# Two ways to lay out the output of a chunked linear recurrence: rows of tokens, or rows of value channels

## The chip, the cores and the metric

One core of one Trainium2 chip runs the whole program. The metric is the device time of one execution in microseconds (us), lower is better. TensorE (PE) multiplies, VectorE (DVE) and ScalarE (ACT) work on tiles in SBUF and in PSUM, GpSimd (POOL) does some small sums, and the queue of SyncE (SP) issues the weight loads. Each engine runs its own instruction list in order; semaphores tie the lists together.

## The reference, cut to what matters

The program is two transformer-like blocks in float32 on 256 tokens of 1024 channels, with some 215 MB of weights read once. The change touches one mixer of the second block, a two-directional gated linear recurrence ("HGRN2") with 4 heads of 128 value channels, in chunks of 32 tokens. It is summed over both directions, normed per token and head, scaled and gated:

```python
def step(state, inp):                     # per chunk of 32 tokens, per head
    qc, kc, vc, gc = inp
    bcum = jnp.cumsum(gc, axis=2)
    btot = bcum[:, :, -1:]
    qe = qc * jnp.exp(bcum)
    ke = kc * jnp.exp(-bcum)
    att = jnp.where(causal_in_chunk, jnp.einsum('bhtk,bhsk->bhts', qe, ke), 0.0)
    o = jnp.einsum('bhtk,bhkv->bhtv', qe, state) + jnp.einsum('bhts,bhsv->bhtv', att, vc)
    ...
def _hg_readout(o, g, norm_w):            # o is the sum of both directions
    o = o * lax.rsqrt(jnp.mean(o * o, axis=-1, keepdims=True) + EPS)
    o = o * norm_w ...
    return o * jax.nn.silu(g)
```

What follows the mixer is a product with an output matrix, and that wants its input with channels on the partitions.

## The kernel before, in words

**Staging.** All weight matrices stream through a ring of 4 raw tiles of 1 MB (`raw`). A list of "units" fixes their order. SP issues the load of a unit as soon as the unit four places ahead of it has been used. For most units ACT then makes a rounded high part (`whi`, line 1053), DVE the low part (`wlo`, line 1582), and PE takes three products per tile (lines 491 to 493). Units of kind "ada" are used raw: 16 small matmul records at line 592, after which ACT copies the bank out (line 1076). SP can load on only when PE has used them.

**The stretch with the recurrence.** After the gates are ready the program goes through eight slots n = 0 to 7, one per direction and head (`SLOT2`). In a slot PE does `within(n)` (line 837, attention inside a chunk), `adds(n)` (line 851, what each chunk adds to the state), `turn_kd` (line 825), and then one projection unit of 48 large matmuls. In the middle of that unit, and at its end in the last slots, it does `outputs(n-1)` (lines 862 and 867). DVE masks the attention (line 1987), runs the recurrence over the 8 chunk states (line 1995), splits weights (line 1582) and takes the output out of PSUM in `keep_o` (lines 1964 and 1966). `within(n)` waits for `keep_o(n-2)`, and `outputs(n)` for the states and for `keep_o(n-1)`.

`outputs` has, for one head and direction, two matmuls for the attention part (one per 128 tokens) and eight for the state part (one per chunk of 32 tokens). Before, the tokens are the rows of the result: the 32 queries of a chunk are the stationary operand and the 128x128 state streams past it. The four chunks of 128 tokens sit in four column groups of the array. A float32 matmul shows as two records in the trace, so these ten matmuls are 4 and 16 records.

**The stretch behind it.** Ten steps s = 0 to 9 of a windowed attention (the `na` steps) follow: scores (line 897), ACT's exponentials (1188), DVE's bias, maximum and scaling (2040 to 2051), PE's transposes (909) and the weighted sums (924). Each step carries up to two "ada" units, and from s = 5 on a projection by the output matrix (`evoB`), which reads the normed and gated recurrence output. The norm of that output runs in the first steps. Before: ACT squares and sums rows (line 1395) as heads become ready, and forms one factor per token and head; DVE applies it (line 2020, s = 0); PE waits for that in s = 1 and turns the result by eight transposes (line 938); DVE multiplies by the gate out of PSUM (line 2026, s = 1); ACT and DVE split it into high and low parts (lines 1458 and 2060, s = 2).

Of the kernel before, what the change touches and what calls it, by code (L numbers as in the profile page):

```python
# [22 lines left out]
P = 128  # L23
D = 1024
KT = D // P
S = 256
# [111 lines left out]
def build(nc, x, norm_gain, w_in, b_forget, lambda_q1, lambda_k1, lambda_q2, lambda_k2, subln_gain, sinks,  # L138
# [25 lines left out]
    with ExitStack() as ctx:  # L164
# [114 lines left out]
        ot = oT[:, :, :].rearrange("p h s -> p (h s)").rearrange("p (t j v) -> p t j v", t=NT, j=4)  # L279
# [206 lines left out]
        def _(pe):  # L486
# [368 lines left out]
            def outputs(n):  # L855
                d, j = 1 - n // 4, n % 4
                pe.wait_ge(att_set, min(n + 2, 8))
                pe.wait_ge(st_set, n + 1)
                if n:
                    pe.wait_ge(o_kept, n)  # L860
                for t in range(NT):
                    mm(psY[:, t * P:(t + 1) * P], ATTM[2 * (n // 4) + n % 2][:, t, :], hv[:, t, j * P:(j + 1) * P],
                       start=(t == 0), stop=False, skip_group_check=True)
                for t in range(NT):
                    for c in range(4):
                        cc = 4 * t + c
                        last = mm(psY[c * CH:(c + 1) * CH, t * P:(t + 1) * P], QE[d][:, j, cc * CH:(cc + 1) * CH],
                                  sq[:, n % 2, cc, :], start=False, stop=True, skip_group_check=True)
                last.then_inc(o_done, 1)
# [58 lines left out]
            for s in range(NA + 2):  # L928
                if s >= 2:
                    na_turn(s - 2, 0)  # L930
                if s < NA:
                    na_scores(s)
                if s == 1:
                    pe.wait_ge(hg_gated, 1)
                    for j in range(4):
                        for t in range(NT):
                            n = (j % 2) * NT + t
                            last = nc.tensor.transpose((psX, psY)[j // 2][:, n * P:(n + 1) * P], ot[:, t, j, :],
                                                       ident[:, :])
                    last.then_inc(sub_sum, 1)  # L940
                ada(f"na{s}a")
                if s >= 2:
                    na_turn(s - 2, 1)
                if s in EVO_AT:
                    if EVO_AT[s] == 0:
                        pe.wait_ge(hg_ready, 1)
                    project(SPAN["evoB"][EVO_AT[s]], Hhi, Hlo, base=4)
                ada(f"na{s}b")
                if s >= 2:
                    na_weigh(s - 2)  # L950
# [81 lines left out]
        def _(act):  # L1032
# [358 lines left out]
            def square_output(j):  # L1391

                act.wait_ge(o_kept, 5 + j)
                for t in range(NT):
                    ins = nc.scalar.activation(kk[:, j // 2, 2 * (j % 2) + t, 0:P], ot[:, t, j, :], ACT.Square,
                                               accum_out=lbc[:, 0, 4 * t + j:4 * t + j + 1])
                return ins

# [12 lines left out]
            for n, u in enumerate(SLOT2):  # L1411
# [18 lines left out]
                else:  # L1430
                    square_output(0)
                    square_output(1)
# [15 lines left out]
            for s in range(NA + 2):  # L1448
                if s >= 2:
                    keep_turned(s - 2, 0)  # L1450
                if s == 0:
                    square_output(2)
                    step(square_output(3))
                    step(nc.scalar.activation(lbc[:, 1, :], lbc[:, 0, :], ACT.Ln, bias=eps[:, 0:1], scale=1.0 / P))
                    nc.scalar.activation(lbc[:, 2, :], lbc[:, 1, :], ACT.Exp, scale=-0.5).then_inc(sub_inv, 1)
                elif s == 2:
                    act.wait_ge(hg_gated, 2)
                    nc.scalar.copy(Hhi[:, 4:8, :], oT[:, :, :]).then_inc(hg_high, 1)
# [3 lines left out]
                if s < NA:  # L1462
                    exps(NG + s, [(pn[:, s % 2, i, :], psS[:, 2 * (s % 2) + i, :]) for i in range(2)], False)
                keep_rows(f"na{s}b")
# [94 lines left out]
        def _(dve):  # L1559
# [398 lines left out]
            def keep_o(n):  # L1958
# [3 lines left out]
                o = psY[:, 0:S].rearrange("p (t v) -> p t v", t=NT)  # L1962
                if n < 4:
                    ins = V.tensor_copy(ot[:, :, j, :], o)
                else:
                    ins = V.tensor_tensor(ot[:, :, j, :], ot[:, :, j, :], o, ALU.add)
# [48 lines left out]
            def scale_output():  # L2015

                dve.wait_ge(sub_inv, 2)
                o = ot.rearrange("p t j v -> p (t j) v")
                r = lbc[:, 2, :].rearrange("p (a b) -> p a b", b=1).to_broadcast([P, 8, P])
                then(V.tensor_tensor(o, o, r, ALU.mult), hg_gated, 1)  # L2020

            def norm_output():

                dve.wait_ge(sub_sum, 3)
                for i, o in enumerate((psX, psY)):
                    ins = V.tensor_tensor(oT[:, 2 * i:2 * i + 2, :], o[:, :].rearrange("p (h s) -> p h s", h=2),
                                          sgh[:, 2 * i:2 * i + 2, :], ALU.mult)
                ins.then_inc(sub_taken, 1)
                dve.wait_ge(sub_taken, 3)
                dve.sem_inc(hg_gated, 1)  # L2030

            dve.wait_ge(nb_set, 1)
            for s in range(NA + 2):
# [19 lines left out]
                if s == 0:  # L2053
                    gate_output()
                    scale_output()
                elif s == 1:
                    norm_output()
                elif s == 2:
# [231 lines left out]
```

## Time and profile before

| | |
|---|---|
| median of 3 runs | 1130.73 us (1130.66 to 1133.12) |
| the profiled execution | 1130.73 us |
| its span, first to last instruction | 1129.0 us |
| granted TensorE clock, mean | 0.995 |
| PE busy / DVE busy / ACT busy | 95% / 65% / 52% of the span |

The span is 1.7 us shorter than the execution that it belongs to; that part lies around the instructions. All times "at" some microsecond below are counted from the span's start. The recurrence slots lie at 478 to 541 us, the windowed attention behind them at 541 to 602 us. Durations of matmul records are modelled and overlap; what a matmul costs is read from the distance of starts.

### The profile page before, as it was taken

Reading aid. Unit: us, or ns where it says so; the run is one execution under the profiler, and the core shown is the slowest. Engines: PE = TensorE matmul, PEld = TensorE weight load, DVE = VectorE, ACT = ScalarE, POOL = GpSimd, SP = SyncE. Lnnn points to the kernel's source line nnn. Section 1 sums busy time; section 2 is a strip of 40 time slices with the busy share of each in tenths; the row PEclk is TensorE's granted clock in tenths of the full one; section 3 lists DMA queues with packets and bytes.
Section 4 is the critical chain, followed back from the end, with each engine's and each line's share of the span. In section 5 each row is a group of like instructions: output and inputs, shape, how many; then the busy total and the mean of one; then the engine's idle time right before and its main releaser. Section 6 shows DMA issues by size and latency. Waiting matters only on the chain.

```text
span 1129.0 us, 22056 instructions
## 1 busy us (share of the span) xinstructions
PE 1077.7 (95%) x9350; PEld 1010.7 (90%) x9350; DVE 735.5 (65%) x1095; ACT 586.3 (52%) x888; POOL 83.9 (7%) x93
## 2 busy tenths in 40 slices
PE   6999999999999989999898999999999989999997
PEld 6988778898989989989567899999989989999997
DVE  6467656654667686795775776774476766767643
ACT  5555654644455564632654755553454455556433
POOL 2000000100201361000111000000010010000000
PEclk9999999999999999999999999999999999999999
DMA  8556565786776585533676655455465567564631
GB/s 268 183 189 234 198 208 184 219 274 217 231 239 201 172 206 164 172 114 113 241 275 231 224 184 190 154 204 203 149 224 187 170 200 256 166 204 165 223 113 38
DMA packets 165774, 219.81 MB, mean 195 GB/s; under 512 B 4481, under 2 KB 146205, under 8 KB 165676
## 3 DMA queue, kind: packets, MB, share of 16 engines
q1 hardware_dynamic: 164442, 215.67, 58.2%
q0 software_dynamic: 832, 1.65, 0.7%
q8 instruction: 74, 1.21, 0.4%
q10 hardware_dynamic: 402, 1.08, 0.4%
q14 instruction: 24, 0.20, 0.1%
HBM read 217.27 MB, written 1.11 MB: 193 GB/s over the span
## 4 chain that ended last, share of the span: by engine, by line
PE 47%; DVE 5%; ACT 2%; DMA 1%; issue 1%; DVEq 0%; ACTq 0%
PE psG L491 11%; PE psG L493 10%; PE psG L492 10%; PE psS L493 4%; PE psS L491 4%; PE psS L492 4%; PE psG L592 1%; DVE wlo L1582 1%; ACT whi L1053 1%; PE psY L617 1%; DVE Hlo L1647 1%; DMA raw<-in_ev_w_out_dram 1%; DMA raw<-in_ffn_w_up_dram 1%; DVE vt L1638 0%; DVE stat L2042 0%
## 5 line engine op out<-in xcount | busy, mean ns | idle before, releaser
L1582 DVE TENSOR_TENSOR wlo<-raw,whi 128x1024 fp32r<-128x1024 f32 x311 | 376.2, 1245 | 155.4 <-ACT whi L1053 150.4
L491 PE MATMUL psG<-Hlo,whi 128*128 128x256 f32 x1520 | 436.8, 287 | 12.9 <-DVE wlo L1582 5.2
L493 PE MATMUL psG<-Hhi,whi 128*128 128x256 f32 x1520 | 429.3, 282 | 0.0
L492 PE MATMUL psG<-Hhi,wlo 128*128 128x256 f32 x1520 | 429.0, 282 | 0.0
L1053 ACT CAST whi<-raw 128x1024 fp32r<-128x1024 f32 x311 | 316.1, 1048 | 123.5 <-PE psS L493 68.3
L491 PEld LDWEIGHTS psG<-Hlo,whi 128*128 128x128 f32 x1520 | 287.6, 189 | 21.7 <-issue 10.5
L492 PEld LDWEIGHTS psG<-Hhi,wlo 128*128 128x128 f32 x1520 | 287.9, 189 | 0.1
L493 PEld LDWEIGHTS psG<-Hhi,whi 128*128 128x128 f32 x1520 | 287.4, 189 | 0.0
L491 PE MATMUL psS<-Glo,whi 128*128 128x256 f32 x352 | 99.5, 283 | 0.0
L492 PE MATMUL psS<-Ghi,wlo 128*128 128x256 f32 x352 | 99.1, 282 | 0.0
L493 PE MATMUL psS<-Ghi,whi 128*128 128x256 f32 x352 | 99.1, 282 | 0.0
L492 PEld LDWEIGHTS psS<-Ghi,wlo 128*128 128x128 f32 x352 | 66.3, 188 | 0.1
L491 PEld LDWEIGHTS psS<-Glo,whi 128*128 128x128 f32 x352 | 66.3, 188 | 0.1
L493 PEld LDWEIGHTS psS<-Ghi,whi 128*128 128x128 f32 x352 | 66.3, 188 | 0.0
L2080 DVE SCALAR_TENSOR_TENSOR fz<-fa,pcol,fz 128x255 f32<-128x255 f32 x52 | 25.1, 483 | 59.9 <-ACT fz L1493 59.0
L1510 ACT COPY fa<-psG 128x512 f32<-128x512 f32 x22 | 12.9, 585 | 93.0 <-PE psG L493 93.0
L491 PE MATMUL psG<-Xlo,whi 128*128 128x256 f32 x192 | 55.4, 288 | 1.1 <-issue 0.7
L493 PE MATMUL psG<-Xhi,whi 128*128 128x256 f32 x192 | 54.0, 281 | 0.0
L492 PE MATMUL psG<-Xhi,wlo 128*128 128x256 f32 x192 | 54.0, 281 | 0.0
L592 PE MATMUL psG<-raw,cs 128*32 128x256 f32 x768 | 51.9, 394 | 1.5 <-ACT sg L1171 0.8
L2195 POOL TENSOR_TENSOR arow<-arow 128x512 f32<-128x512 f32 x12 | 15.5, 1288 | 505.2 <-ACTq L1080 505.2
L1076 ACT COPY arow<-psG 128x256 f32<-128x256 f32 x48 | 17.8, 370 | 51.9 <-PE psG L592 51.7
(378 smaller groups left out, 1654.8 us busy)
## 6 DMA issues: line engine op xcount, KB each, us to landing
raw<-in_ada_w_dram SPq DMA_DIRECT2D x48, 1024.0 KB, 5.5
raw<-in_ffn_w_up_dram SPq DMA_DIRECT2D x44, 1024.0 KB, 5.1
raw<-in_w_in_dram SPq DMA_DIRECT2D x29, 1024.0 KB, 6.9
raw<-in_ev_w_in_dram SPq DMA_DIRECT2D x26, 1024.0 KB, 5.6
raw<-in_ffn_w_down_dram SPq DMA_DIRECT2D x22, 1024.0 KB, 4.8
raw<-in_od_w_in_dram SPq DMA_DIRECT2D x12, 1024.0 KB, 5.2
raw<-in_w_in_dram SPq DMA_DIRECT2D x9, 512.0 KB, 6.1
raw<-in_w_o_dram SPq DMA_DIRECT2D x4, 1024.0 KB, 7.9
```

The source lines that it names most:

```text
L491: mm(o, a_hi, b_lo, start=first, stop=False, skip_group_check=shared)
L492: mm(o, a_lo, b_hi, start=False, stop=False, skip_group_check=shared)
L493: return mm(o, a_hi, b_hi, start=False, stop=last, skip_group_check=shared)
L592: last = mm(bank(u)[32 * j:32 * j + 32, 0:256], cs[:, UNITS[u][2] + k, :], w[:, k, j * 256:(j + 1) * 256], start=(k == 0), stop=(k == 1))
L617: last = mm(psY[:, 0:S], ones[:, 0:P], sqv[:, k, :], start=False, stop=(k == KT - 1))
L1053: nc.scalar.copy(ring_half(whi, v, i), src).then_inc(hi_split, 1)
L1076: nc.scalar.copy(ada_row(n)[:, q * 256:(q + 1) * 256], bank(u)[:, 0:256]).then_inc(bank_free[B0[u] % 2], 1)
L1510: nc.scalar.copy(fa[:, i % 2, :, :], src).then_inc(bank_free[B0[ua] % 2], 1)
L1582: V.tensor_tensor(ring_half(wlo, v, h - H0[v]), src, ring_half(whi, v, h - H0[v]).bitcast(F32), ALU.subtract).then_inc(lo_split, 1)
L1647: ins = V.scalar_tensor_tensor(lo[:, m, :], VALUE[m % 3], shift[:, m:m + 1], hi[:, m, :].bitcast(F32), ALU.add, ALU.subtract)
L2080: step(V.scalar_tensor_tensor(z[:, q, 1:S], src[:, q, 0:S - 1], pcol[:, w[0] + q:w[0] + q + 1], z[:, q, 1:S], ALU.mult, ALU.add))
L2195: step(G.tensor_tensor(r[:, 0:512], r[:, 0:512], r[:, 512:1024], ALU.add))
```

## The change

The recurrence output is formed with value channels as rows from the start. In `outputs` the two operands of each matmul trade places: `hv` and the states `sq` are stationary (128 columns each), the masked attention and the queries stream (128 and 32 columns). The eight transposes are dropped. The per-token sum of squares is now across partitions, so it is done by two matmuls with a matrix of ones, after one ACT square of the whole output; ACT forms the factor for all rows (`Ln`, then `Exp`, both of full width) and DVE multiplies twice.

```diff
@@ outputs (PE)
                 for t in range(NT):
-                    mm(psY[:, t * P:(t + 1) * P], ATTM[2 * (n // 4) + n % 2][:, t, :], hv[:, t, j * P:(j + 1) * P],
-                       start=(t == 0), stop=False, skip_group_check=True)
-                for t in range(NT):
+                    mm(psY[:, t * P:(t + 1) * P], hv[:, t, j * P:(j + 1) * P], ATTM[2 * (n // 4) + n % 2][:, t, :],
+                       start=True, stop=False)
                     for c in range(4):
                         cc = 4 * t + c
-                        last = mm(psY[c * CH:(c + 1) * CH, t * P:(t + 1) * P], QE[d][:, j, cc * CH:(cc + 1) * CH],
-                                  sq[:, n % 2, cc, :], start=False, stop=True, skip_group_check=True)
+                        last = mm(psY[:, cc * CH:(cc + 1) * CH], sq[:, n % 2, cc, :],
+                                  QE[d][:, j, cc * CH:(cc + 1) * CH], start=False, stop=(c == 3))
@@ na steps (PE), s == 1
-                    pe.wait_ge(hg_gated, 1)
-                    ... 8 transposes of ot into psX and psY
+                    pe.wait_ge(sub_sq, 2)
+                    for i, o in enumerate((psX, psY)):
+                        last = mm(o[:, :], ones[:, 0:P], kd[:, 2 * i:2 * i + 2, :], start=True, stop=True)
                     last.then_inc(sub_sum, 1)
@@ ACT: square_output (8 squares with row sums) and the two small Ln and Exp are gone
                 if s == 0:
+                    act.wait_ge(o_kept, 8)
+                    nc.scalar.activation(kd[:, :, :], oT[:, :, :], ACT.Square).then_inc(sub_sq, 1)
-                elif s == 2:
-                    act.wait_ge(hg_gated, 2)
+                elif s == 3:
+                    act.wait_ge(hg_gated, 1)
                     nc.scalar.copy(Hhi[:, 4:8, :], oT[:, :, :]).then_inc(hg_high, 1)
...
+                if s == 1:
+                    act.wait_ge(sub_sum, 3)
+                    for i, o in enumerate((psX, psY)):
+                        ins = nc.scalar.activation(headr2[:, 2 * i:2 * i + 2, :], o[:, :].rearrange(
+                            "p (h s) -> p h s", h=2), ACT.Ln, bias=eps[:, 0:1], scale=1.0 / P)
+                    ins.then_inc(sub_taken, 1)
+                    act.wait_ge(sub_taken, 3)
+                    nc.scalar.activation(headr2, headr2, ACT.Exp, scale=-0.5).then_inc(sub_inv, 1)
@@ DVE: scale_output (s == 0) and the old norm_output (s == 1, out of PSUM) become, at s == 2
+                dve.wait_ge(sub_inv, 2)
+                step(V.tensor_tensor(oT[:, :, :], oT[:, :, :], headr2, ALU.mult))
+                then(V.tensor_tensor(oT[:, :, :], oT[:, :, :], sgh[:, :, :], ALU.mult), hg_gated, 1)
@@ DVE: the low part of the output moves from s == 2 to s == 3
```

On PE, in the middle of a projection unit, one `outputs` reads as follows in the instruction order. A name before the comma streams, the name behind it is stationary, and the shape is rows of the result by streamed columns; `hov` and `qke` hold queries.

```order
 L492 MATMUL psG<-Xhi,wlo 128x256
 L493 MATMUL psG<-Xhi,whi 128x256
-L862 MATMUL psY<-hv,sgh 128x128 x2
-L867 MATMUL psY<-sq,hov 32x128 x8
+L862 MATMUL psY<-sgh,hv 128x128
+L866 MATMUL psY<-hov,sq 128x32 x4
+L862 MATMUL psY<-sgh,hv 128x128
+L866 MATMUL psY<-hov,sq 128x32 x4
 L491 MATMUL psG<-Xlo,whi 128x256
```

The number of matmuls stays ten. The state matmuls have 128 rows and 32 streamed columns instead of 32 rows and 128 columns, and the attention part of the second 128 tokens comes behind the first four of them.

On PE around step s = 1 of the windowed attention, before:

```order
L897 MATMUL psS<-nak,naq 128x256 x2
L897 MATMUL psS<-cnk,naq 128x256 x2
L938 MATMUL psX<-ident,oT 128x128 x4
L938 MATMUL psY<-ident,oT 128x128 x4
L592 MATMUL psG<-raw,cs 32x256 x16
L909 MATMUL psX<-ident,pn 128x128 x4
```

And now:

```order
L896 MATMUL psS<-nak,naq 128x256 x2
L896 MATMUL psS<-cnk,naq 128x256 x2
L935 MATMUL psX<-kd,ones 128x512
L935 MATMUL psY<-kd,ones 128x512
L592 MATMUL psG<-raw,cs 32x256 x16
L908 MATMUL psX<-ident,pn 128x128 x4
```

The two sums of squares stand where the transposes stood. The transposes of the attention weights (line 909, now 908) overwrite `psX`, so they now wait for ACT's `Ln` where they waited for DVE's product.

On DVE, steps s = 0 to 2 before, from the gate to the low part of the output:

```order
L2011 SCALAR_TENSOR_TENSOR sgh<-sgh,pcol,hq 128x256 x4
L2020 TENSOR_TENSOR oT<-oT,lbc 128x1024
L2040 TENSOR_TENSOR psS<-psS,tok 128x256 x2
L2042 TENSOR_REDUCE stat<-psS 128x2
L2048 RECIPROCAL stat<-stat 128x2
L2051 TENSOR_SCALAR pn<-pn,stat 128x512 x2
L2026 TENSOR_TENSOR oT<-psX,sgh 128x512
L2026 TENSOR_TENSOR oT<-psY,sgh 128x512
L2040 TENSOR_TENSOR psS<-psS,tok 128x256 x2
```

And now, from step s = 1 to the low part in step s = 3:

```order
L2031 TENSOR_SCALAR pn<-pn,stat 128x512 x2
L2020 TENSOR_TENSOR psS<-psS,tok 128x256 x2
L2022 TENSOR_REDUCE stat<-psS 128x2
L2028 RECIPROCAL stat<-stat 128x2
L2031 TENSOR_SCALAR pn<-pn,stat 128x512 x2
L2009 TENSOR_TENSOR oT<-oT,qke 128x1024
L2010 TENSOR_TENSOR oT<-oT,sgh 128x1024
L2020 TENSOR_TENSOR psS<-psS,tok 128x256 x2
```

Nothing stands between the gate and the next bias any more, and both products stand one and two steps later than their counterparts did.

## Rows read from the trace of the kernel before

**Rows 1.** The page, chain that ended last: shares of the span by engine.

```profile
PE 47%; DVE 5%; ACT 2%; DMA 1%; issue 1%; DVEq 0%; ACTq 0%
```

**Rows 2.** Windows: stretch and its length, busy us per engine, clock, DMA.

```profile
520.00:541.00 21.00, 18.69 (x219) 16.83 (x217) 11.94 (x31) 8.16 (x20) 0.00 (x0) 1.00 0.20 67
548.30:552.00 3.70, 3.65 (x35) 1.63 (x35) 3.28 (x6) 1.79 (x5) 0.00 (x0) 0.54 0.70 242
```

**Rows 3.** Timeline of PE around outputs(0): start, duration, line, tiles, records.

```profile
486.75 0.28 PE L493 MATMUL psG<-Xhi,whi 128*128 128x256 f32 x1
486.87 0.61 PE L862 MATMUL psY<-hv,sgh 128*128 128x128 f32 x4
487.40 0.64 PE L867 MATMUL psY<-sq,hov 128*32 128x128 f32 x16
487.98 0.39 PE L491 MATMUL psG<-Xlo,whi 128*128 128x256 f32 x1
488.20 0.27 PE L492 MATMUL psG<-Xhi,wlo 128*128 128x256 f32 x1
```

**Rows 4.** Timeline of PE's weight loads at a matmul with 8 streamed columns.

```profile
648.96 0.53 PEld L604 LDWEIGHTS psX<-sel,arow 128*128 128x128 f32 x4
649.41 0.19 PEld L491 LDWEIGHTS psG<-Hlo,whi 128*128 128x128 f32 x1
```

**Rows 5.** Groups by line and form: weight loads, busy us and mean ns.

```profile
L862 PEld LDWEIGHTS psY<-hv,sgh 128*128 128x128 f32 x16 | 2.1, 190 | 0.0
L867 PEld LDWEIGHTS psY<-sq,hov 128*32 128x32 f32 x64 | 1.5, 109 | 0.5
```

**Rows 6.** Timeline of PE where within(2), within(3) and within(4) begin.

```profile
490.81 0.28 PE L493 MATMUL psG<-Xhi,whi 128*128 128x256 f32 x1
491.18 0.71 PE L837 MATMUL psY<-hov 128*128 128x128 f32 x4
...
501.25 0.71 PE L837 MATMUL psY<-hov 128*128 128x128 f32 x4 [1.43 <-DVE oT L1964]
...
509.74 0.61 PE L837 MATMUL psY<-qke 128*128 128x128 f32 x4
```

**Rows 7.** The same timeline, from the last outputs to step s = 2.

```profile
539.73 0.68 PE L862 MATMUL psY<-hv,hgt 128*128 128x128 f32 x4 [2.31 <-DVE oT L1966]
...
540.92 0.70 PE L897 MATMUL psS<-nak,naq 64*128 64x256 f32 x4
...
547.24 0.66 PE L938 MATMUL psX<-ident,oT 128*128 128x128 f32 x4 [2.26 <-DVE oT L2020]
...
548.26 3.52 PE L592 MATMUL psG<-raw,cs 128*32 128x256 f32 x32
551.83 0.64 PE L909 MATMUL psX<-ident,pn 128*128 128x128 f32 x4
```

**Rows 8.** Timeline of DVE in the first steps of the windowed attention.

```profile
545.96 1.22 DVE L2020 TENSOR_TENSOR oT<-oT,lbc 128x1024 f32<-128x1024 f32 x1
...
548.02 1.22 DVE L2042 TENSOR_REDUCE stat<-psS 128x2 f32<-128x1024 f32 x1
...
550.39 0.69 DVE L2026 TENSOR_TENSOR oT<-psX,sgh 128x512 f32<-128x512 f32 x1
```

**Rows 9.** Groups by form: the first block's sum of squares by ones.

```profile
L753 PE MATMUL psX<-tok,ones 128*128 128x512 f32 x4 | 2.3, 644 | 0.0
```

**Rows 10.** Timeline of ACT: the first block's Ln and Exp; exponentials of step s = 1.

```profile
143.35 0.69 ACT L1215 ACTIVATE tok<-psX,eps 128x512 f32<-128x512 f32 x1
144.07 1.06 ACT L1219 ACTIVATE tok<-tok 128x1024 f32<-128x1024 f32 x1
...
550.58 0.69 ACT L1188 ACTIVATE pn<-psS,stat 128x512 f32<-128x512 f32 x1
```

**Rows 11.** Chain that ended last, in order of time, before the first evoB unit.

```profile
561.44 7.36 DMA raw<-in_ev_w_out_dram
568.87 1.05 ACT whi L1053
```

More of the change, by code:

```diff
@@ L278, in build @@
         headr = tok[:, 1, :].rearrange("p (a b) -> p a b", a=2)
-        ot = oT[:, :, :].rearrange("p h s -> p (h s)").rearrange("p (t j v) -> p t j v", t=NT, j=4)
+        headr2 = qke[:, 0, :, :]
         nbA = tok[:, :, :].rearrange("p t n -> p (t n)")[:, 0:5 * 6 * HD].rearrange(
@@ L933, in _ @@
                 if s == 1:
-                    pe.wait_ge(hg_gated, 1)
[L935 to L939, printed above, removed]
+                    pe.wait_ge(sub_sq, 2)
+                    for i, o in enumerate((psX, psY)):
+                        last = mm(o[:, :], ones[:, 0:P], kd[:, 2 * i:2 * i + 2, :], start=True, stop=True)
                     last.then_inc(sub_sum, 1)
@@ L1389, in keep_query @@
                 keep(u, naq[:, 2 * n:2 * n + 2, :], SCALE)
[L1391 to L1397, printed above, removed]
             nc.scalar.preload_act_table_set(TABLES)
@@ L1430, in _ @@
                 else:
-                    square_output(0)
-                    square_output(1)
                     act.wait_ge(f_mul, 4)
@@ L1451, in _ @@
                 if s == 0:
[L1452 to L1455, printed above, removed]
-                elif s == 2:
-                    act.wait_ge(hg_gated, 2)
+                    act.wait_ge(o_kept, 8)
+                    nc.scalar.activation(kd[:, :, :], oT[:, :, :], ACT.Square).then_inc(sub_sq, 1)
+                elif s == 3:
+                    act.wait_ge(hg_gated, 1)
                     nc.scalar.copy(Hhi[:, 4:8, :], oT[:, :, :]).then_inc(hg_high, 1)
@@ L1961, in keep_o @@
                 dve.wait_ge(o_done, n + 1)
-                o = psY[:, 0:S].rearrange("p (t v) -> p t v", t=NT)
                 if n < 4:
-                    ins = V.tensor_copy(ot[:, :, j, :], o)
+                    ins = V.tensor_copy(oT[:, j, :], psY[:, 0:S])
                 else:
-                    ins = V.tensor_tensor(ot[:, :, j, :], ot[:, :, j, :], o, ALU.add)
+                    ins = V.tensor_tensor(oT[:, j, :], oT[:, j, :], psY[:, 0:S], ALU.add)
                 then(ins, o_kept, n + 1)
@@ L2013, in gate_output, with norm_output @@
                 step(ins)
-            def scale_output():
+            def norm_output():
                 dve.wait_ge(sub_inv, 2)
[L2018 to L2030, printed above, removed]
+                step(V.tensor_tensor(oT[:, :, :], oT[:, :, :], headr2, ALU.mult))
+                then(V.tensor_tensor(oT[:, :, :], oT[:, :, :], sgh[:, :, :], ALU.mult), hg_gated, 1)
             dve.wait_ge(nb_set, 1)
@@ L2054, in _ @@
                     gate_output()
-                    scale_output()
-                elif s == 1:
+                elif s == 2:
                     norm_output()
-                elif s == 2:
+                elif s == 3:
                     dve.wait_ge(hg_high, 1)
```

## The prediction

> **What bounds the kernel now.** I read the page's chain of waits first. Of the time it puts down to an engine most is PE's, and DVE's share is small [rows 1]; the reader should take from it only that an instruction added to PE counts unless PE waits at that place. So the second view is the table by stretches, for the two places that the change touches. In the last slots of the recurrence the load queues are busy for 0.20 of the time only, the clock is full, and PE is busy for 18.69 of 21 us, DVE for 11.94 [rows 2]: PE is the bound there, and no load. The third view is PE's timeline, to find where it waits. In the slots it waits three times that matter: shortly before within(2), for 1.43 us before within(3), where it is DVE that is late [rows 6], and for 2.31 us before outputs(7) [rows 7]. Between them one slot runs into the next. In the steps behind, PE waits 2.26 us for DVE's scaling before the transposes, and the 32 ada records behind them take 3.52 us [rows 7] at a granted clock of 0.54 [rows 2], that is, nearly all at the lower of the two levels, 1.2 GHz; at the upper, 2.4, they would take 3.52 x 0.54 = 1.9 us. The fourth view is the chain in order of time: it leaves these steps through the load of the first evoB unit, ACT's and DVE's split of it [rows 11]. What PE wins earlier in these steps has to get past that.
>
> **outputs, what it costs before.** From the first L862 (486.87) to the second matmul of the resumed projection (488.20) are 1.33 us, of which one projection slot of 0.12 (486.75 to 486.87) belongs to L491. So one outputs takes 1.21 us for 20 records [rows 3]. The 16 state records start within 0.58 us, 0.036 us each: four column groups share the array.
>
> **outputs, what it costs after.** The records stay 20, but each state record now loads 128 stationary columns and streams 32. No row of the kernel has this form. From above in streamed columns: a record of L862 loads 128 columns and streams 128, and with the switch to four column groups behind it the four take 0.53 us, at most 0.13 each [rows 3]. From below: L604 loads 128 and streams 8, and its four loads take 0.45 us to the next load (648.96 to 649.41), 0.112 each [rows 4]. Both ends lie close together, so it is the load that sets the pace; weight loads of 32 columns take 109 ns and of 128 columns 190 [rows 5], 81 ns more. I take 0.112, the row with few columns: 20 x 0.112 = 2.25 us, 1.04 more than now. The low end would be that the four-fold overlap survives and an outputs costs what it does now or less, by the 0.1 us twice lost at the switch between array forms; the high end is a load that can't lie beside the streaming at all, 0.112 plus a quarter of 0.112 for 32 of 128 columns, 0.45 us more per outputs.
>
> The first L867 starts 0.53 us after the first L862, where four records at 0.112 would be 0.45 [rows 3]: changing the array's form costs something. The Trainium skill, "TensorEngine Tiling (Array Packing)", section "Key Properties", says the same ("Mode switching requires drain"), and it would make the new form cheaper; its section "When to Use Tiling" goes against the change, since for a moving operand of 32 columns it advises to swap the operands and tile the columns four times, which is the layout that is given up. By the rows the drains are some 0.2 us against 1.24 us of lost packing, so the second rule outweighs the first.
>
> **Where it counts.** outputs(0) and (1) each delay PE by 1.04. Before within(2) PE is idle from 490.93 (490.81 and one slot) to 491.18, 0.25 us; before within(3) it has 1.43 us plus the 0.16 by which a modelled end (0.28) exceeds a slot (0.12), 1.59 us [rows 6]. Both waits are for DVE, whose list there is full and doesn't wait for the two outputs. They swallow 1.84 of 2.08, 0.24 is left. outputs(2) to (5) find no wait at within(4) [rows 6] or later: 4 x 1.04 = 4.16. Behind outputs(6) PE waits 2.31 us for DVE's recurrence [rows 7], which doesn't need it: hidden. If that cover were gone it would cost 1.04. outputs(7) is on the path at once: from 539.73 to 540.92 it takes 1.19 now [rows 7], then 2.25 and a switch of form to the scores, 0.1: +1.1. The sum at the first scores is 0.24 + 4.16 + 1.1 = 5.5 us later.
>
> **The norm.** ACT's eight small squares, their two small functions and their waits go; one square over 128x1024 comes. That is as large as the Exp in [rows 10], 1.06 us, and ends about 1.1 us behind keep_o(7), well before PE has done scores(1). So PE's 2.26 us wait goes, and with it probably the lower clock. The ones matmuls cost 1.9 us (four records over about 2.3 us in two separate pairs [rows 9], with one start less) against 1.0 for the transposes (547.24 to 548.26 [rows 7]). What is late next: the transposes of line 909 now wait for ACT's two Ln of 0.69 us [rows 10], which stand behind the exponentials of s = 1, which stand behind DVE's maximum. Without L2020 that maximum ends at 549.24 - 1.22 = 548.0 on the old clock [rows 8]; two exponentials and two Ln of 0.69 [rows 10] take to 550.9 with their starts. PE is ready at 544.98 (547.24 less its wait) + 1.9 for the ones + 1.9 for ada = 548.8, waits 2.2 us again, and begins these transposes at 551.0 instead of 551.83 [rows 7]. A stall of 2.26 us is traded for one of 2.2 us, and of 3 us on paper 0.8 us are won.
>
> On DVE the products cost 2 x 1.22 instead of 1.22 + 2 x 0.69 [rows 8], 0.16 less, but they and the low part come later, in s = 2 and 3, where PE's steps follow one another closely. By s = 4 DVE has the same work behind it as before, and is no more than 0.16 us earlier, except for what of its waits for PE closes. ACT's split of the first evoB unit [rows 11] can't come before the exponentials of s = 4, which need DVE. The load itself should land 1 to 2 us earlier, since ada units are used earlier; only 0.3 us of that gets past ACT and DVE. I take 0.3 us as won, with 3 us won and (rival 4) 1.5 us lost as the ends.
>
> **Sum.** 1130.7 + 5.5 - 0.3 = 1135.9 us. The sum is against the profiled execution of 1130.73, which is also the median of the runs shown. All later phases hang on the ring of loads and on PE, and should only be shifted.
>
> **Rivals.**
> 1. *The stall's time gets through.* If DVE and ACT keep up, the 2.26 us wait and the excess of the 32 ada records (3.52 against 1.9), less 0.9 us for the larger matmuls, reach evoB: -3.0 instead of -0.3, 1133.2. For it: the load of that unit takes 7.36 us and sets its split [rows 11], so an earlier issue helps it. Against it: the new wait for Ln, and that ACT's split stands behind exponentials that wait for DVE. 12%.
> 2. *The overlap stays, and the kernel is faster.* If loads of 128 columns for short streams overlap like those of L867, 0.036 us a record, an outputs is 0.45 + 0.58 = 1.0 us, 0.2 less than now; five of them on the path give -1.0, with the norm's -0.3 to -3.0: 1129.4 to 1126.7, say 1128.5 or less. It decides at outputs(2), where PE has no wait, and holds only if a state record costs under about 0.06 us. Against it stands L604's 0.112 [rows 4]. 7%.
> 3. *Load and stream in a row.* 0.45 us more for each outputs: 0.9 in the first two, 1.8 in four, 0.45 in the last, together 3.1: 1139.0. The Trainium skill, "TensorE: Matmul & The Clock Gate", section "Part 3: Packing small matmuls — row/col tiling", says that a load overlaps matmuls in flight only when the row group differs, which would give this. By that rule L862, with all 128 rows in each record, would take about twice 0.11, and the trace has at most 0.13 [rows 3]; the rule doesn't hold for this form here. 8%.
> 4. *The norm loses.* The new 2.2 us wait before line 909 brings the lower clock down on scores(2) and the ada units behind it; they would take some 2 us more, against 0.8 won: up to 1.5 us late at keep_na, 1137.4. 13%.
> My forecast holds the other 60%, with a range of its own of 1134.8 to 1136.9.
>
> **Chances and range.** About 0.3% (3.4 us, the limit 1134.1) is what a measurement can tell from no change. The forecast and rivals 3 and 4 are slower by more: 0.60 + 0.08 + 0.13, and a little of rival 1, less a little of the forecast: 0.80. Same: rival 1 and part of rival 2, 0.14. Faster: 0.06. The range runs from 1132.0, below rival 1, to 1139.0, rival 3.
>
> **What the changed profile would show.** Weight loads of L866 start 0.112 us apart, 16 of them, with a mean of about 190 ns; an outputs takes 2.2 us; within(3) starts about 0.2 us later without a wait worth the name; the first scores stand at 546.4. PE has no wait before the ones matmuls, and one of about 2 us before line 908, put down to ACT's Ln. The evoB split stands 5.2 us later than before. The prediction is wrong if L866 runs at clearly less than 0.1 us a record, if PE waits more than 0.5 us in slots 3 to 6, or if evoB's split moves by less than 4 us.

## The result, and the profile after

| | before | after |
|---|---|---|
| median | 1132.64 us | 1142.68 us |
| lowest to highest | 1130.66 to 1134.43 | 1139.74 to 1144.45 |
| the profiled execution, its span | 1130.73, 1129.0 | 1138.87, 1137.1 |

The change makes the kernel slower: the ratio is 1.0096 with a 95% interval of 1.0079 to 1.0114, that is 10.9 us (8.9 to 12.9), where 5.2 were predicted, and 1142.7 us lies above the range. Run once more as it is (`after_again` below) it gave 1.0094 [1.0078, 1.0111]. Both profiled executions are faster than their medians, by 1.9 us before and 3.8 us after, so the pair of profiles is 8.1 us apart and can't show all of the loss.

The chain's shares by engine, which answer to [rows 1], look quite different:

```profile
PE 75%; DVE 14%; ACT 6%; issue 2%; DMA 2%; SPq 0%; POOL 0%; DVEq 0%; ACTq 0%
```

I don't build on that: the chain follows one releaser at each step. What can be compared are starts. In the profile of after everything ahead of within(1) is 0.65 us early (480.69 against 481.34), before any changed instruction counts. Shifts are therefore counted from within(1) of each profile. Here are outputs(0) and the starts of within(3) and (4) on PE's timeline, the answer to [rows 3, 6]:

```profile
486.11 0.28 PE L493 MATMUL psG<-Xhi,whi 128*128 128x256 f32 x1
486.23 0.38 PE L862 MATMUL psY<-sgh,hv 128*128 128x128 f32 x2
486.44 0.98 PE L866 MATMUL psY<-hov,sq 128*128 128x32 f32 x8
487.26 0.47 PE L862 MATMUL psY<-sgh,hv 128*128 128x128 f32 x2
487.56 0.98 PE L866 MATMUL psY<-hov,sq 128*128 128x32 f32 x8
488.38 0.37 PE L491 MATMUL psG<-Xlo,whi 128*128 128x256 f32 x1
488.58 0.28 PE L492 MATMUL psG<-Xhi,wlo 128*128 128x256 f32 x1
...
500.71 0.62 PE L837 MATMUL psY<-hov 128*128 128x128 f32 x4
...
510.15 0.61 PE L837 MATMUL psY<-qke 128*128 128x128 f32 x4
```

One outputs takes 486.23 to 488.58, less a slot of 0.12: 2.23 us. within(3) starts without a wait, 0.11 later than before; within(4) starts 9.44 us behind it, where that was 8.49 [rows 6]. The same timeline from the last outputs to step s = 2, against [rows 7]:

```profile
543.19 0.46 PE L862 MATMUL psY<-hgt,hv 128*128 128x128 f32 x2 [1.18 <-DVE oT L1957]
543.48 1.18 PE L866 MATMUL psY<-qke,sq 128*128 128x32 f32 x8
544.47 0.77 PE L862 MATMUL psY<-hgt,hv 128*128 128x128 f32 x2
545.04 1.75 PE L866 MATMUL psY<-qke,sq 128*128 128x32 f32 x8
546.72 1.23 PE L896 MATMUL psS<-nak,naq 64*128 64x256 f32 x4
...
548.73 2.99 PE L592 MATMUL psG<-raw,cs 128*32 128x256 f32 x32
551.66 0.70 PE L896 MATMUL psS<-nak,naq 64*128 64x256 f32 x4
...
552.72 1.12 PE L935 MATMUL psX<-kd,ones 128*128 128x512 f32 x2
553.68 1.02 PE L935 MATMUL psY<-kd,ones 128*128 128x512 f32 x2
...
559.12 0.63 PE L908 MATMUL psX<-ident,pn 128*128 128x128 f32 x4 [2.56 <-ACT qke L1451]
```

The two halves of outputs(7) are not alike: the first L866 has 1.18 us, the second 1.75. What happened there shows in the table by stretches (length, busy us of the engines, granted clock):

```profile
520.00:541.00 21.00, 21.00 (x210) 20.26 (x209) 11.32 (x31) 6.00 (x9) 0.00 (x0) 1.00 0.22 75
543.20:551.70 8.50, 8.50 (x62) 5.96 (x62) 3.10 (x6) 1.99 (x3) 0.00 (x0) 0.60 0.01 3
```

In the first row PE has no gap (21.00 of 21). Before it was busy for 18.69 [rows 2]; the difference is the wait of 2.31 us ahead of outputs(7) [rows 7], which lay inside that stretch. Now it is 1.18 us long and lies behind the stretch's end, so the two rows don't compare the slots themselves. From outputs(7) to scores(1) the granted clock is 0.60, so mostly the lower level, 1.2 GHz. In the kernel before, the same work had 1.00:

```profile
539.70:544.00 4.30, 4.27 (x62) 2.68 (x64) 2.19 (x4) 3.21 (x12) 0.00 (x0) 1.00 0.01 4
```

DVE's timeline from the maximum of step s = 1 to the low part, for [rows 8]:

```profile
553.71 1.22 DVE L2022 TENSOR_REDUCE stat<-psS 128x2 f32<-128x1024 f32 x1
...
560.94 0.76 DVE L2020 TENSOR_TENSOR psS<-psS,tok 128x256 f32<-128x256 f32 x2 [4.89 <-PE psS L896]
...
564.11 1.23 DVE L2009 TENSOR_TENSOR oT<-oT,qke 128x1024 f32<-128x1024 f32 x1
565.37 1.23 DVE L2010 TENSOR_TENSOR oT<-oT,sgh 128x1024 f32<-128x1024 f32 x1
...
569.81 1.23 DVE L2039 TENSOR_TENSOR Hlo<-oT,Hhi 128x1024 fp32r<-128x1024 f32 x1
```

And ACT's timeline from step s = 1 to the first evoB split, for [rows 10, 11]:

```profile
555.83 0.37 ACT L1072 COPY arow<-psG 128x256 f32<-128x256 f32 x1 [2.84 <-PE psG L592]
556.23 0.69 ACT L1184 ACTIVATE pn<-psS,stat 128x512 f32<-128x512 f32 x1
...
557.72 0.69 ACT L1451 ACTIVATE qke<-psX,eps 128x512 f32<-128x512 f32 x1
...
577.30 1.04 ACT L1049 CAST whi<-raw 128x1024 fp32r<-128x1024 f32 x1
```

DVE stands idle for 4.89 us while PE waits for ACT, and then has bias, maximum, both products and the low part one behind the other. ACT's Ln stands behind the exponentials, and these behind a copy that waits for PE's ada unit. The split by ACT starts at 577.30, before at 568.87 [rows 11]; with the 0.65 us of the start that is 9.1 us later.

**Where the time went, in this pair of profiles** (us later, from within(1)):

| piece | shift | predicted |
|---|---|---|
| start of outputs(7) | 4.11 | 4.40 |
| outputs(7) itself: 3.53 (543.19 to 546.72) against 1.19 | 2.34 | 1.1 |
| scores(0) and 32 ada: 4.94 (546.72 to 551.66) against 2.93 | 2.01 | 0 |
| scores(1) to the transposes of line 908 | -0.52 | -0.8 |
| from there to evoB's split: 18.18 (559.12 to 577.30) against 17.04 | 1.14 | 0.5 |
| sum | 9.1 | 5.2 |

The 2.93 are the start of the second scores before (543.85, between the rows of [rows 7]) less 540.92. The last two entries under "predicted" are the prediction's 0.8 us won before line 909 (now 908), and the part of it that it did not let get through.

### The profile page after: what moved, and what is told of

Same layout as the page of the kernel before. It is cut to its first block, busy times and chain, and to the rows that moved or that the text cites. A ratio compares the mean times of both kernels' runs of the same rounds, so it can differ in the third digit from the quotient of the medians.

```text
span 1137.1 us, 22032 instructions
## 1 busy us (share of the span) xinstructions
PE 1086.0 (96%) x9346; PEld 1019.8 (90%) x9346; DVE 736.1 (65%) x1094; ACT 586.3 (52%) x874; POOL 84.1 (7%) x93
## 4 chain that ended last, share of the span: by engine, by line
PE 75%; DVE 14%; ACT 6%; issue 2%; DMA 2%; SPq 0%; POOL 0%; DVEq 0%; ACTq 0%
PE psG L491 18%; PE psG L493 18%; PE psG L492 18%; DVE wlo L1574 4%; PE psS L491 4%; PE psS L492 4%; PE psS L493 4%; PE psG L592 2%; ACT whi L1049 2%; DMA raw<-in_w_in_dram 2%; PE psY L866 1%; PE psY L617 1%; DVE Hlo L1639 1%; PE psS L696 1%; DVE vt L1630 1%
## 5 line engine op out<-in xcount | busy, mean ns | idle before, releaser
L491 PE MATMUL psG<-Hlo,whi 128*128 128x256 f32 x1520 | 435.3, 286 | 14.2 <-DVE wlo L1574 5.7
L491 PEld LDWEIGHTS psG<-Hlo,whi 128*128 128x128 f32 x1520 | 286.4, 188 | 23.2 <-issue 10.1
L491 PE MATMUL psS<-Glo,whi 128*128 128x256 f32 x352 | 99.4, 282 | 0.0
L491 PEld LDWEIGHTS psS<-Glo,whi 128*128 128x128 f32 x352 | 66.3, 188 | 0.1
L1502 ACT COPY fa<-psG 128x512 f32<-128x512 f32 x22 | 12.9, 586 | 93.0 <-PE psG L493 93.0
L491 PE MATMUL psG<-Xlo,whi 128*128 128x256 f32 x192 | 55.2, 288 | 1.1 <-issue 0.7
```

Of the source, the lines that this page charges most:

```text
L491: mm(o, a_hi, b_lo, start=first, stop=False, skip_group_check=shared)
L1502: nc.scalar.copy(fa[:, i % 2, :, :], src).then_inc(bank_free[B0[ua] % 2], 1)
```

## The experiments

All ratios are to the kernel before, with their 95% intervals. The theory: the outputs cost their slower pace, and on top the clock falls behind PE's remaining wait ahead of outputs(7); the norm wins nothing because DVE and ACT get its work late. Rivals: the loss comes from the norm alone; the pace of the outputs is set by something other than the load; the low clock comes of the thin streams and not of the wait.

**The two halves of the change, apart.** `outputs_only` is the kernel before with the new outputs, whose norm goes on as if rows were tokens; `norm_only` is the kernel after with the old outputs, whose norm goes on as if rows were channels.

```diff
 (outputs_only, on before)
-   mm(psY[:, t * P:(t + 1) * P], ATTM[...][:, t, :], hv[:, t, ...], ...)
+   mm(psY[:, t * P:(t + 1) * P], hv[:, t, ...], ATTM[...][:, t, :], ...)
-   mm(psY[c * CH:(c + 1) * CH, t * P:(t + 1) * P], QE[d][...], sq[:, n % 2, cc, :], ...)
+   mm(psY[:, cc * CH:(cc + 1) * CH], sq[:, n % 2, cc, :], QE[d][...], ...)
 (norm_only, on after: the same lines the other way round)
```

> The kernel before with only the ten matmuls of each outputs in the new form; norm, transposes and gate as before (their values are then laid out wrongly, their times are not changed by that). Theory 1, that the trace of the changed kernel shows the outputs as the main cost and the low clock that falls inside outputs(7) as a consequence of it: first scores 6 to 6.5 us later than before against the same point of the slots, scores and ada behind them slow again by about 2 us, total 7 to 9 us slower than before. Theory 2, my prediction's sum without a clock term: 5.5 us slower, and outputs(7) takes 2.3 us at full clock. Each L866 record 0.11 us from the next in both.

> The changed kernel with outputs in the old form (its result is then laid out wrongly for the norm; times are not changed by that). Theory 1: the new norm by itself loses, because PE's wait only moves from DVE's scaling to ACT's Ln, and both full-width products and the low part stand later on DVE, just before the first evoB unit: 0 to 2 us slower than before. Theory 2, my prediction: 0.3 us faster. Rival 1 of the prediction, the stall's time gets through: 3 us faster.

Measured: `outputs_only` 1.0065 [1.0041, 1.0090], 7.4 us; `norm_only` 1.0026 [1.0012, 1.0039], 2.9 us. Together 10.3, within the interval of the whole. The time of `outputs_only` doesn't exclude the 5.5 us of the second theory; its profile does: outputs(7) takes 2.96 us (543.24 to 546.20) and the scores and 32 ada records behind it 5.53 (to 551.73), where before has 1.19 and 2.93. In `outputs_only` the first scores stand 5.85 us later than before and evoB's low part 6.6; in `norm_only` 1.5 and 3.3, of which 1.5 is a stretch of lower clock inside the slots, 502.2 to 505.6 us, that after itself doesn't have. It begins 1.6 us behind the end of a 1.45 us wait ahead of within(3), with matmuls of 256 streamed columns on PE. So the outputs are the larger loss, and the norm in this place is a loss too (1.4 to 4.4 us by the interval), not the small gain of the forecast.

**Is the load the pace?** `narrow16` is after with half of each chunk's columns streamed; the other half of the output is left out.

```diff
-   mm(psY[:, cc * CH:(cc + 1) * CH], sq[...], QE[d][:, j, cc * CH:(cc + 1) * CH], ...)
+   mm(psY[:, cc * CH:cc * CH + 16], sq[...], QE[d][:, j, cc * CH:cc * CH + 16], ...)
```

> The changed kernel with 16 instead of 32 streamed columns in each state matmul (half of the tokens' state part left out). If the load of 128 stationary columns sets the pace: L866 records still 0.11 us apart, an outputs 2.2 us, total as the changed kernel within 1 us. If streaming has a share: records 0.1 us apart or less and 1 to 2 us faster.

Measured: 1.0082 [1.0061, 1.0103]. Its outputs(0) on PE's timeline:

```profile
487.95 0.38 PE L862 MATMUL psY<-sgh,hv 128*128 128x128 f32 x2
488.17 0.96 PE L866 MATMUL psY<-hov,sq 128*128 128x16 f32 x8
488.98 0.47 PE L862 MATMUL psY<-sgh,hv 128*128 128x128 f32 x2
489.29 0.96 PE L866 MATMUL psY<-hov,sq 128*128 128x16 f32 x8
490.10 0.36 PE L491 MATMUL psG<-Xlo,whi 128*128 128x256 f32 x1
```

From the first L862 to L491 are 2.15 us, as with 32 columns (486.23 to 488.38, 2.15). Half the columns give nothing back in an outputs, so the streamed columns don't set the pace, and a load and a stream don't lie in a row. (The total is 1.6 us below after's by the ratios, and the intervals overlap, so it says nothing of so small a difference.) The load of 128 stationary columns is what is left and fits; a fixed time for each full-array record would fit as well, and no run here changes the load alone. The weight loads of L866 and L862 in after have nearly the same mean, where four-column-group loads had 109 ns [rows 5]:

```profile
L866 PEld LDWEIGHTS psY<-hov,sq 128*128 128x128 f32 x64 | 7.8, 192 | 0.0
...
L862 PEld LDWEIGHTS psY<-sgh,hv 128*128 128x128 f32 x16 | 2.4, 190 | 0.0
```

**The wait before outputs(7).** `after_filler` puts work whose result nobody reads into that wait; `outputs_filled` does the same to `outputs_only`.

```diff
+   for i in range(9):
+       mm(psX[:, 0:S], Xhi[:, i % KT, 0:P], Xhi[:, i % KT, :], start=True, stop=True)
    outputs(7)
```

> The changed kernel plus 9 full matmuls (128 rows, 256 columns, 0.12 us each) into the free bank psX, between outputs(6) and outputs(7), where PE waits 1.18 us for DVE. Theory A, the clock falls because of that wait: it stays at 2.4 GHz through outputs(7) and the scores, outputs(7) takes 2.3 instead of 3.5 us and the 32 ada records 1.9 instead of 2.9: about 3 us faster than the changed kernel. Theory B, it falls because outputs(6) and (7) stream only 32 columns under loads of 128: it falls all the same, no change within 0.5 us.

> outputs_only (new outputs, old norm) plus 9 full matmuls of 0.12 us in PE's wait before outputs(7). If the extra over my term of 5.5 us is the clock that falls in that wait: outputs(7) takes 2.3 us, the first scores come 5 to 5.5 us later than before in the slots' own time, total 5 to 6 us slower than before, 1.0045 to 1.0055. If the extra has another cause: as outputs_only, 1.0065.

Measured: `after_filler` 1.0054 [1.0038, 1.0071], `outputs_filled` 1.0043 [1.0030, 1.0056]. Nine matmuls more on the engine that bounds the kernel, and it runs about 4.7 us faster (0.0042 of 1132.6; the intervals of 1.0096 and 1.0054 don't meet), where 3 were expected. For `outputs_filled` against `outputs_only` the gain is 2.5 us, and there the intervals overlap. The work fits into the wait: from the last L866 group of outputs(6) to outputs(7) are 2.16 us with it and without it (542.23 to 544.39, and 541.03 to 543.19 in after). PE's timeline of `after_filler`:

```profile
543.04 1.31 PE L884 MATMUL psX<-Xhi 128*128 128x256 f32 x9
544.39 0.46 PE L862 MATMUL psY<-hgt,hv 128*128 128x128 f32 x2
...
546.71 0.70 PE L898 MATMUL psS<-nak,naq 64*128 64x256 f32 x4
...
547.77 1.93 PE L592 MATMUL psG<-raw,cs 128*32 128x256 f32 x32
...
557.10 0.63 PE L910 MATMUL psX<-ident,pn 128*128 128x128 f32 x4 [2.55 <-ACT qke L1453]
```

Its table by stretches (length, busy us, granted clock after POOL's):

```profile
543.00:557.00 14.00, 11.52 (x115) 7.39 (x114) 8.18 (x17) 7.34 (x16) 0.00 (x0) 1.00 0.51 180
558.00:561.40 3.40, 3.40 (x25) 1.40 (x22) 1.77 (x3) 0.89 (x3) 1.99 (x2) 0.50 0.92 361
```

outputs(7) is 544.39 to 546.71, 2.32 us and not 3.53; the ada records take 1.93 and not 2.99; the clock is 1.00 throughout. The second row is the price that remains: behind the 2.55 us wait for ACT the clock falls here, where in after it stayed. Of the six profiles with this wait, four have the fall within 1.5 us of its end (`after_filler`, `narrow16`, `old_last_two`, `norm_only`) and two don't (`after`, `after_again`). In `outputs_filled`, whose norm is the old one, the first scores stand 5.19 us later than before and evoB's split 5.04: this is what the outputs cost by themselves.

The three profiles with the nine matmuls (the third is below) have 1.00 at outputs(7); the five with a thin form of outputs(7) (few streamed columns in each matmul) and an open wait (`outputs_only`, `after`, `after_again`, `early_norm`, `narrow16`) all fall at 543.8 to 545.1 us, between 0.1 us before and 1.6 us behind the start of outputs(7). PE's timeline of `after_again` for one:

```profile
544.93 0.77 PE L862 MATMUL psY<-hgt,hv 128*128 128x128 f32 x2 [1.19 <-DVE oT L1957]
...
551.32 3.64 PE L592 MATMUL psG<-raw,cs 128*32 128x256 f32 x32
```

Its table by stretches shows 9.9 us at half the clock. Here the clock falls at 544.80, before the first thin matmul of outputs(7), and the loss is 4.7 us where it is 3.2 in after (outputs(7) 4.38 us, scores and ada 5.58, from the starts):

```profile
544.90:554.80 9.90, 9.87 (x60) 6.91 (x60) 3.61 (x8) 2.50 (x5) 0.00 (x0) 0.50 0.08 11
```

**Is it the thin streams?** `old_last_two` is after with the old form for outputs(6) and (7), whose part of the output is then in the old layout.

```diff
-   (new form for every n)
+   if n < 6: (new form)
+   else:     (old form)
```

> The changed kernel with outputs(6) and (7) in the old form (layout of these two heads wrong, times not changed by that). Theory A, the wait lowers the clock: the wait is longer now, 2.3 us, the clock falls in outputs(7) or right behind it; only the 1.1 us of outputs(7) is won. Theory B, the thin streams lower it: the clock stays up until the first scores are done, about 4 us faster than the changed kernel.

Measured: 1.0077 [1.0057, 1.0097]. PE's timeline:

```profile
544.37 0.68 PE L871 MATMUL psY<-hv,hgt 128*128 128x128 f32 x4 [2.31 <-DVE oT L1967]
```

The table by stretches:

```profile
545.00:548.40 3.40, 3.40 (x29) 1.99 (x32) 0.61 (x2) 1.06 (x1) 0.00 (x0) 0.51 0.03 7
```

The clock falls without a thin outputs(7), so the form isn't needed for the fall; the low stretch is 3.4 us and not 6.8 or more. The time decides nothing: 2.1 us faster than after, with intervals that overlap. Before, the same form behind the same 2.31 us did not fall there in its profile. That isn't a difference between the kernels: `late_turn` (next) has the same instructions as before up to the second scores, and in its profile the clock does fall there.

```profile
539.10 0.68 PE L862 MATMUL psY<-hv,hgt 128*128 128x128 f32 x4 [2.31 <-DVE oT L1966]
```

Its table by stretches:

```profile
540.70:544.10 3.40, 3.40 (x32) 1.52 (x32) 2.15 (x4) 1.39 (x8) 0.00 (x0) 0.50 0.02 5
```

So behind the open wait with the old form the clock fell in two profiles of four (`old_last_two` and `late_turn`, not `before` and `norm_only`), for 3.4 us each time; with the new form it fell in five of five, for 6.8 to 10.2 us. Whether it falls varies from execution to execution, and so few profiles don't give a frequency. With work in the wait the clock stayed up in all four profiles.

**Was the removed stall ever a cost?** `late_turn` is before with the eight transposes moved behind the two ada units of the step; `late_turn_filled` has eight matmuls of ones ahead of outputs(7) too.

```diff
-   if s == 1: (wait for hg_gated, eight transposes)
    ada(f"na{s}b")
+   if s == 1: (wait for hg_gated, eight transposes)
 (late_turn_filled, besides)
+   for i in range(8):
+       mm(psX[:, 0:S], ones[:, 0:P], ones[:, :], start=True, stop=True)
    outputs(7)
```

> The kernel before with its eight transposes of step s = 1 put behind the two ada units of that step, so that PE has work while DVE scales. Theory 1, that time won before line 909 is lost again on DVE before the first evoB unit: PE's 2.26 us wait goes, line 909 begins 1 to 3 us earlier, but the total is within 1 us of before. Rival (the stall's time gets through): 2 to 3 us faster than before.

> late_turn plus eight float32 matmuls of ones (0.22 us each) into the free bank psX in PE's wait of 2.31 us before outputs(7). If PE's waits bring the low clock on in some executions, the mean granted clock of its runs rises above that of before and of late_turn, and the time falls by half of the low time avoided, 0.5 to 1.5 us against late_turn. If the clock doesn't depend on them, no difference.

Measured: `late_turn` 0.9998 [0.9986, 1.0011], `late_turn_filled` 1.0011 [0.9995, 1.0027]: no change either, so moving the wait gains nothing. (The profile of `late_turn` is no clean pair to that of before: besides the low stretch shown above it has one of 6.8 us behind the wait for DVE's products, 550.9 to 557.7, and evoB's split stands 3.2 us later. The medians decide here, with a mean granted clock of 0.994 over the runs of both.) The second run did not turn out as expected. The mean granted clock over its runs is 0.994, as in `late_turn` and before, and the expected rise and gain did not come. Its eight matmuls are 16 records and take 3.55 us (536.73 to 540.28), longer than the wait, so outputs(7) starts 1.2 us later than before, counted from within(1). In its profile, though, the clock is full from outputs(7) on and the wait ahead of the transposes is gone, and evoB's split still stands 0.95 us later than before: the late start, less 0.15 to 0.2 us. Its rows on PE's timeline:

```profile
547.72 0.66 PE L948 MATMUL psX<-ident,oT 128*128 128x128 f32 x4
...
552.31 0.63 PE L911 MATMUL psX<-ident,pn 128*128 128x128 f32 x4 [3.50 <-DVE oT L2028]
```

The stretch in the table by stretches, clock 1.00:

```profile
539.00:556.00 17.00, 13.26 (x158) 8.17 (x160) 11.55 (x20) 9.62 (x27) 2.00 (x2) 1.00 0.65 248
```

PE gets the transposes done and then waits 3.50 us for DVE's products. In before the last product runs to 551.68, and line 909 starts at 551.83 [rows 7]. DVE's timeline there:

```profile
551.00 0.68 DVE L2026 TENSOR_TENSOR oT<-psY,sgh 128x512 f32<-128x512 f32 x1
```

It ends 0.15 us before PE goes on. So the 2.26 us wait and the 1.6 us that the low clock added to the 3.52, which the change was to give back, lay beside DVE's list; some 0.2 us could be won from them at most, by this profile.

**The norm in another order.** `early_norm` is after with ACT's Ln and Exp ahead of its copies of ada banks and the exponentials of s = 1, DVE's products a step earlier, and both parts of the split a step earlier. `early_norm_filled` adds the nine matmuls.

```diff
 ACT:
+   if s == 1: (wait for sub_sum; Ln, Ln, Exp)
    keep_rows(f"na{s}a")
-   elif s == 3: (Hhi)
+   elif s == 2: (Hhi)
 DVE:
-   norm_output at s == 2, low part at s == 3
+   norm_output at s == 1, low part at s == 2
```

> The changed kernel with the norm's functions moved up by a place: ACT does Ln and Exp in step s = 1 before its exponentials instead of behind them, DVE multiplies at the end of s = 1, and high and low parts are made in s = 2 as before. Theory 1, that the norm's loss is the wait for Ln (2.56 us) plus DVE's two products in the crowded steps while DVE stood idle for 4.89 us before: 2 to 3 us faster than the changed kernel. Rival, that the norm's loss is only an effect of the clock: no difference beyond 1 us.

> The changed kernel with both mends, the norm's functions a place earlier and 9 full matmuls in the wait before outputs(7). Theory 1, three causes that add up (longer outputs, low clock behind the wait, late norm): only the longer outputs are left, 4.5 to 6 us slower than before, 1.004 to 1.0055, and no wait before line 908. If one of the mends only moved the loss: 1.006 or more.

Measured: `early_norm` 1.0060 [1.0039, 1.0082], `early_norm_filled` 1.0026 [1.0011, 1.0040]. The first is 4.1 us faster than after by the ratios, the second 3.2 us faster than `after_filler`; in both pairs the intervals just touch. The second is also faster than its expectation of 1.004 to 1.0055, which had the norm win nothing. PE's timeline of the latter:

```profile
553.45 0.66 PE L910 MATMUL psX<-ident,pn 128*128 128x128 f32 x4 [0.40 <-DVE pn L2033]
```

And the stretch, again at 1.00:

```profile
542.00:554.00 12.00, 11.56 (x116) 7.30 (x114) 7.98 (x17) 6.39 (x13) 0.00 (x0) 1.00 0.46 166
```

The wait ahead of these transposes is 0.40 us, for DVE's scaled weights, and no longer 2.56 us for ACT. Counted from within(1), the first scores stand 5.19 us later than before, the transposes 2.53 and the evoB low part 3.20: the norm in this order wins back 2 of the 5.2 us that the outputs cost. It is the fastest version with the new outputs, and still 3 us slower than before.

**The change once more**, for the size itself:

> The changed kernel once more, on the chip of the next two, for a second profile and to pair them. Both theories: 1.008 to 1.011 of before; the low clock lies again around outputs(7) and the first scores.

Measured: 1.0094 [1.0078, 1.0111]; the shifts from within(1) are 4.06 at within(7), 7.25 at the first scores and 10.6 at the evoB low part. The mean granted clock over its runs is 0.992, and 0.994 for the runs of before beside them; `early_norm_filled` has 0.996 beside the same runs, and `after_filler` 0.995 beside runs of before with 0.995.

## Why the prediction was wrong, point by point

1. *An outputs takes 2.25 us, the load sets the pace*: the price is right, 2.23 measured, and `narrow16` shows that the streamed columns don't count; that it is the load is the explanation left, not one that a run isolated. The value from [rows 4], a record with only 8 columns, held for 32. The Trainium skill, "TensorEngine Tiling (Array Packing)", section "When to Use Tiling", advises for such matmuls the layout that was given up, and the trace agrees: without the fourfold column tiling an outputs costs 1.02 us more. The rule of the Trainium skill, "TensorE: Matmul & The Clock Gate", section "Part 3: Packing small matmuls — row/col tiling", that a load overlaps a matmul in flight only in another row group (rival 3, 1139.0) does not hold for these records: L866 has all rows in each, and its records start 0.11 us apart with 32 and with 16 streamed columns, where load and stream in a row would have made 2.7 us of an outputs.
2. *Where it counts*: right. within(3) 0.11 later (0.24 predicted), then 1.0 a slot, 4.11 at outputs(7) (4.40). With the clock kept up (`outputs_filled`) the first scores stand 5.19 us later, where the sum has 5.5.
3. **The step that failed first: outputs(7) "+1.1", and all behind it at the clock of before.** The prediction saw that "behind outputs(6) PE waits 2.31 us" and counted it as cover alone: 1.04 hidden. It said that the stall's lower clock would "probably" go, and never asked whether the wait of 1.2 us that is left, ahead of thin work, would bring one down elsewhere. In all five profiles of the new outputs with that wait open the clock fell there. In after that is +1.24 us in outputs(7) and +2.01 in the scores and ada behind it, 3.2 us together; in `after_again` it is 4.7, and the 32 ada records alone took 3.64 us, which take 1.93 at the full clock. Filling the wait takes the ratio from 1.0096 to 1.0054. Rival 4 had the mechanism, but only at the second wait, where it came in four of six profiles and not in after; it gave it 1.5 us and 13%. (By its own terms rival 4 is 1130.7 + 5.5 + 1.5 = 1137.7, not 1137.4.)
4. **The step that failed second: the norm "0.3 us won".** The stall itself was sized about right: of 3 us on paper 0.3 were to get through, and 0.2 or less did, since DVE was as late as PE (`late_turn`, `late_turn_filled`). But "By s = 4 DVE has the same work behind it as before" was wrong in time: DVE idled 4.89 us before 560.94, and what stood on the far side of that idle time, 2.46 us of products, came onto the path: +1.14 in the profile against -0.52 won before it, 0.6 lost where 0.3 was to be won. A cause of the idle time is a row that the step left out: the exponentials of s = 1 stand behind ACT's copy of the ada bank, 555.83, not only behind DVE's maximum, which ended at 554.93. `norm_only` says +2.9 us, its lower clock at 502 included. Moving the work (`early_norm_filled`) turns the loss into a gain of 2 us in the profile, so it was the order and not the amount of the work that lost.
5. *The tell-tales*: the wait before line 908 of about 2 us, put down to ACT's Ln (2.56), came; "the first scores stand at 546.4" (546.72) looks right only because the profile started 0.65 early: the shift is 6.45 and not 5.5. "evoB split 5.2 later" failed at 9.1. None of the three signs of being wrong came, because none of them looks for a loss larger than the forecast.
6. *Rival 1* (1133.2) and *rival 2* (faster) are out, by `late_turn` and `late_turn_filled` and by the 2.23 us.

The direction and the greater part of the outputs' cost were forecast; the missing 5 to 6 us are the clock (3.2 and 4.7 in the two profiles of the change, 4.7 by the ratios of after and `after_filler`) and the norm (about 1 in the profile). What stays open: what decides in which executions the clock falls behind an open wait, since the same instructions kept it in `before` and lost it in `late_turn`, and so how often before itself pays for it. That the low stretch is longer with thin work behind the wait was seen in all five profiles, but not separated from the length of that work, or from the thin outputs(6) ahead of the wait.

## What to carry to other kernels

A wait that swallows an added cost isn't free cover: look what the engine does right behind it, and price that work at the lower clock as well as the upper. A stall is worth something only if the engine it waits for is early afterwards; put the next consumer's start beside that engine's last instruction (551.83 and 551.68 here) before counting it. And when work changes engines, follow it past every copy in the new engine's list: here the norm's products were 0.16 us shorter in sum, and lost time because they came later.

## What the runs showed of the hardware that was not expected

In all five profiles with thin work behind it, a wait of 1.18 to 1.20 us came with the lower clock, from 0.1 us before the wait's end to 1.6 us behind it, for 6.8 us in after (544.1 to 550.9) and 10.2 us in `after_again`. Nine full matmuls of 128x128 by 256, 1.35 us of PE with no use for the result, kept it at 1.00 in all three kernels that had them, and a kernel of 1142.7 us ran about 4.7 us faster for it. In `late_turn_filled` filler won nothing (1.0011 [0.9995, 1.0027]): it was 1.2 us longer than the wait, and in its profile, at full clock from 539 to 556 us, PE only waited longer for DVE. The fall is not a fixed property of a kernel: the same instructions behind the same 2.31 us wait kept the clock in one profile and lost it for 3.4 us in another.
